# Moving one group of matmuls behind tile 0's last products in a projection that is called three times

## The reference

```
h = x + rms_norm(moba_attention(rms_norm(x)), ...)          # 8 heads; w_qkv, w_o
h = h + rms_norm(square(relu(rms_norm(h) @ w_up)) @ w_down)
h = h + gate * hgrn2_mixer(modulate(h))                      # linear recurrence; w_in, w_out
h = h + gate * swiglu(modulate(h))                           # ffn_w_in, ffn_w_out, layer 0
h = h + gate * nsa_mixer(modulate(h), shared_kv)             # 16 heads, 4 kv heads; w_q, w_kv, w_out
h = h + gate * swiglu(modulate(h))                           # layer 1
```

## Time and profile before

| | |
|---|---|
| time, median of 3 runs | 999.04 us (997.88 to 999.96) |
| the profiled execution's own time | 999.59 us |
| its span, from first to last instruction | 997.7 us |
| TensorE busy | 977.8 us, 98% |
| VectorE, ScalarE, POOL busy | 733.2, 521.7, 129.7 us |
| mean granted clock of TensorE | 0.999 |
| share of the last chain of waits | PE 79%, DVE 8%, DMA 5%, ACT 3% |

### The profile page before, as it was taken

The page is one execution under the profiler, slowest core; times in us unless marked ns, Lnnn a source line. Parts: engine busy times, 40 slices in busy tenths (PEclk is TensorE's granted clock), DMA queues, the critical chain, the costliest instruction groups (busy, mean ns, idle before and its releaser), DMA issues.

```text
span 997.7 us, 14897 instructions
## 1 busy us (share of the span) xinstructions
PE 977.8 (98%) x5482; PEld 800.0 (80%) x5482; DVE 733.2 (73%) x1086; ACT 521.7 (52%) x733; POOL 129.7 (13%) x163
## 2 busy tenths in 40 slices
PE   8999999999999999999999999999999999999998
PEld 6777788888887888887878888878877778888886
DVE  5787777787678979887878686999768876545454
ACT  6637375445455585873454344456277544434341
POOL 1000100000001000762400000014913120000000
PEclk9999999999999999999999999999999999999999
DMA  9991669799736979006799989658240328555541
GB/s 344 369 354 57 209 259 372 265 368 383 267 113 219 367 264 369 8 32 203 240 381 336 330 297 330 231 183 262 86 170 3 128 86 273 191 188 181 197 158 53
DMA packets 113796, 227.66 MB, mean 228 GB/s; under 512 B 5041, under 2 KB 58561, under 8 KB 113745
## 3 DMA queue, kind: packets, MB, share of 16 engines
q1 hardware_dynamic: 112192, 222.34, 62.2%
q0 software_dynamic: 1408, 4.54, 1.6%
q10 hardware_dynamic: 144, 0.10, 0.1%
HBM read 225.90 MB, written 1.06 MB: 227 GB/s over the span
## 4 chain that ended last, share of the span: by engine, by line
PE 79%; DVE 8%; DMA 5%; ACT 3%; issue 2%; SPq 1%; POOL 1%; DVEq 0%; ACTq 0%; POOLq 0%
PE psum L1980 74%; DMA adaw<-in_ada_w 2%; DVE wlo L1298 1%; DMA raw<-in_attn_w_qkv 1%; DMA raw<-in_ffn_w_in 1%; PE psum L2630 1%; DVE adaw L1319 1%; PE psum L2495 1%; PE psum L1998 1%; DVE arena L1418 1%; DMA raw<-in_attn_w_o 1%; ACT whi L791 1%; DVE res L1427 1%; PE psum L2358 1%; SPq L432 1%
## 5 line engine op out<-in xcount | busy, mean ns | idle before, releaser
L1298 DVE TENSOR_TENSOR wlo<-raw,whi 128x2048 fp32r<-128x2048 f32 (+1 forms) x156 | 310.3, 2005 | 137.4 <-ACT whi L791 137.1
L1980 PE MATMUL psum<-whi,xhi 128*128 128x512 f32 x888 | 350.7, 397 | 5.2 <-DVE xlo L1382 2.1
L1980 PE MATMUL psum<-whi,xlo 128*128 128x512 f32 x888 | 344.9, 390 | 0.0
L791 ACT CAST whi<-raw 128x2048 fp32r<-128x2048 f32 (+1 forms) x157 | 262.6, 1683 | 157.4 <-PE psum L1980 102.1
L1980 PE MATMUL psum<-wlo,xhi 128*128 128x512 f32 x888 | 343.4, 390 | 0.0
L1980 PEld LDWEIGHTS psum<-whi,xhi 128*128 128x128 f32 x888 | 166.7, 188 | 44.3 <-issue 6.5
L1980 PEld LDWEIGHTS psum<-whi,xlo 128*128 128x128 f32 x888 | 166.7, 188 | 35.5
L1980 PEld LDWEIGHTS psum<-wlo,xhi 128*128 128x128 f32 x888 | 166.9, 188 | 32.7
L1319 DVE SCALAR_TENSOR_TENSOR adaw<-adaw,crow 128x1024 f32<-128x1024 f32 x112 | 131.9, 1222 | 3.2 <-DMA adaw<-in_ada_w 3.0
L1980 PE MATMUL psum<-whi,hhi 128*128 128x512 f32 x296 | 115.4, 390 | 0.0
L1980 PE MATMUL psum<-whi,hlo 128*128 128x512 f32 x296 | 115.2, 389 | 0.0
(11 more groups left out here) (284 smaller groups left out, 987.4 us busy)
## 6 DMA issues: line engine op xcount, KB each, us to landing
adaw<-in_ada_w SPq DMA_DIRECT2D x48, 1024.0 KB, 6.9
raw<-in_ffn_w_in SPq DMA_DIRECT2D x88, 512.0 KB
raw<-in_ffn_w_out SPq DMA_DIRECT2D x44, 512.0 KB
raw<-in_w_up SPq DMA_DIRECT2D x16, 1024.0 KB
raw<-in_w_down SPq DMA_DIRECT2D x16, 1024.0 KB
raw<-in_hgrn_w_in SPq DMA_DIRECT2D x16, 1024.0 KB
raw<-in_attn_w_qkv SPq DMA_DIRECT2D x10, 1024.0 KB
adaw<-in_kv_ada_w SPq DMA_DIRECT2D x8, 1024.0 KB, 9.4
```

The costliest lines, as they stand in the source:

```text
L791: sc.copy(whi[:, s, 0:width], raw[:, s, 0:width]).then_inc(hi_ready[s], 1)
L1298: ve.tensor_tensor(wlo[:, s, 0:width], raw[:, s, 0:width], whi[:, s, 0:width].bitcast(F32), ALU.subtract).then_inc(lo_ready[s], 1)
L1980: return te.matmul(dst, lhsT, rhs, start=start, stop=stop, skip_group_check=open_)
```

## The change

In `accumulate` the second slot's products of tile 1, `part(1, 1)`, are issued between the two passes of the last loop instead of ahead of it. The order of the last five groups was: slot 1 tile 0, slot 1 tile 1, tile 0 slots 2 and 3, tile 1 slots 2 and 3. It becomes: slot 1 tile 0, tile 0 slots 2 and 3, slot 1 tile 1, tile 1 slots 2 and 3. The matmuls themselves, their operands and the semaphores that they raise are the same; `part(1, 1)` is what raises `used[1]`. Nothing changes on the other engines.

```
@@ -2120,8 +2120,9 @@
                 part(1, 0)
                 if late is not None:
                     late(3)
-                part(1, 1)
                 for i in range(TT):
+                    if i == 1:
+                        part(1, 1)
                     for f in range(2):
                         for s in (2, 3):
                             item_ready(s, n)
```

## The result

The changed kernel takes 1018.12 us (median of 4 runs, 1017.38 to 1019.91) against 999.08 before: 19.0 us more, ratio 1.0194 with a 95% interval of 1.0176 to 1.0212. It is slower, as forecast, by 19.0 instead of 16.5 us. The profiled execution has a span of 1016.9 us, 19.2 over the one before.

The account below looks back on a forecast made before the run. TensorE, busy for 98% of the span, was taken as the bound. Waits of 3.1 + 5.7 + 5.7 = 14.5 us plus 2.0 for one clock fall gave 16.5 us, 1015.5 on the median; range 1011.5 to 1019.5.

Parts of the forecast that it names:

- the queue behind `used[1]`: All three projections: late copy of slot 1 delays tile 0's post-processing in in-order lists, so TensorE waits; 14.5 us.
- First projection, 3.1 forecast: Attention output projection: TensorE waits 3.1 us at tile 0's transposes, behind slot 1's late copy and subtraction.
- Second, 5.7 for the copy: Recurrent mixer's projection: slot 1's copy, on the chain of waits, comes 5.44 + 0.3 late; cost 5.7 us.
- The price of a fall there, taken as 2.0: Second projection: clock falls during the wait, slowing eight transposes and six products; 2.0 us, the only fall counted.
- Third, 5.7 for the copy: Second attention's projection: copy 7.8 late, but VectorE's subtraction of slot 1 and the transposes 5.7 late; cost 5.7 us.
- The wait of 2.4 for slot 3: Third projection: tile 0's slot 3 products, wanted earlier, wait 2.4 us for VectorE's subtraction.
- The 2.4 is not added again: Third projection: the wait for slot 3 adds nothing to the 5.7 us, since the chain doesn't pass it twice.
- The rival with a fall in the third: Clock falls in the third projection too: 18.5 us, 1017.5; chance 0.27 for falls in more than one place.
- The rival with all three falls: Clock falls in all three projections, 1.0 us in the first: 19.5 us, 1018.5; within the same 0.27 chance.
- Downstream is rigid: MLP loops: each load and product is released by the one before, so delays aren't given back.
- The swallowing of the second's delay: Rival: a later load wait absorbs the second projection's 5.7 us; 8.8 us in all, 1007.8; chance 0.08.
- The rival on the other side: Faster: tile 0's sums, 2.7 us earlier, close TensorE's gaps before the transposes; 2.4 us gained, 996.6; chance 0.03.

Follow-up runs that it names:

- first_only: New order of products in the first projection only, the other two as in the kernel before: 1001.61 us, 3.6 over before.
- filled: Changed kernel plus products of constants in TensorE's long waits of the second and third projection: 1013.89 us, 15.9 over before.
- the changed kernel again: The changed kernel run once more without further edits, as base for comparisons: 1018.55 us, 20.1 over before.
- third_mended: Changed kernel with slot 1's copy and subtraction behind tile 0's post-processing, and the third's slot 3 subtraction ahead of the last turned low half: 998.93 us.
- lists_moved: Changed kernel with slot 1's copy (ScalarE) and subtraction (VectorE) moved behind tile 0's post-processing steps in all three projections: 1001.49 us, 3.1 over before.
- third_only: New order of products in the third projection only, the other two as in the kernel before: 1005.77 us, 7.8 over before.
- half: Against the kernel before, the moved group stands behind tile 0's first half of the columns only, in all three projections: 1006.34 us, 7.9 over before.

## Why the prediction was right, and where it was short

- What bounds the kernel, and the queue behind `used[1]`: right. Moving the two lists, with the new order of products kept, takes back 17 of 20 us.
- First projection, 3.1 forecast: 3.04 of idle in the profile, and 3.2 on the path (118.31 - 116.64 = 1.67, and the 1.5 by which the stretch began earlier). The run of its own gave 3.6, with an interval of 2.3 to 5.0 and a fall in it.
- Second, 5.7 for the copy: 5.8. Of the 0.3 in it for slot 3's late start only 0.1 was read from a row; the slot's products came 453.74 - 1.71 - 451.77 = 0.26 late. The price of a fall there, taken as 2.0: tile 1's transposes are 479.99 - 470.42 = 9.57 later and tile 0's 7.52, so 2.05. The load behind it took 10.51 us instead of 10.07, 0.4 that wasn't in the sum.
- Third, 5.7 for the copy: 7.2. The wait of 2.4 for slot 3 was forecast, and is 2.20. The step that was short is "The 2.4 is not added again", with the clock counted for the waits at the transposes alone. The prediction weighed standstills against the 2.7 us that the clock took to fall at the end of the kernel, and left this shorter one out. But behind this wait, too, the clock fell, and 30 products took 8.72 us instead of 7.10. That is 1.6 in front of the copy, where every us counts.
- "I count the fall in the second projection and leave the others to the rivals": the term that was too small. Behind the third's transposes it fell as well: 830.43 against 811.23 is 19.20, tile 0's 17.16, so 2.0. The rival with a fall in the third named 1017.5, without the one inside the stretch. In the profiled execution 2.05 + 1.6 + 2.0 = 5.7 us are the clock's, and 4.2 by the fillers over several executions; 2.0 had been forecast. The queue's part of the sum was right in size: 3.2 + 5.8 + 5.6 = 14.6, forecast 14.5.
- In the first, no fall was counted. The profiled execution had none (1.06 behind 3.04 us), but three others did (`first_only`, `filled`, the changed kernel again), for 0.5 to 1.4 us. The forecast's 1.0 for that fall was about right, its probability too low. The rival with all three falls named 1018.5, against 1018.12 measured. That closeness is partly luck: in the profiled execution its 1.0 in the first projection is missing, and 1.6 that it didn't have stands in the third.
- The sum of the profiled execution: 3.2 + 5.8 + 2.05 + 0.4 + 7.2 + 2.0 = 20.7, less 1.5 by which it reached the first projection earlier, is the 19.2 of the spans.
- Downstream is rigid, and the loads keep their distance: right. The swallowing of the second's delay didn't happen: the load wait moved from 488.64 to 498.21, by 9.57 like tile 1's transposes, and grew by 0.4.
- The rival on the other side, that the early sums close TensorE's gaps, failed on the lists as said. `third_mended`, where the lists no longer stand in the way, is worth at most 1.3 us by its interval, not 2.4. The gap before tile 1's transposes of the first projection stays (1.22 us). Those before tile 0's in the second and third (0.40 and 0.63 us by the brackets of the timeline before; the prediction's 0.56 was counted from start to start) do close, but behind them TensorE waits 0.47 and 0.45 us for tile 0's low halves, and in the third 0.86 us ahead of them.

## What to carry to other kernels

When a group of products is moved, look first at which semaphore its last product raises and at what stands behind the wait on it in the in-order lists of the other engines. Results that come earlier help only if the lists let them be used; results that come later can hold up everything behind the wait, related or not. Where two lists are coupled, change them together: the moved lists alone cost 4 us, the moved products alone 19, both together 3, and with slot 3's subtraction mended too nothing that can be measured. Here a wait of 2 to 6 us on TensorE cost, besides its own length on the path, up to 2 us more behind it through the clock, in some executions and not in others.

## What the runs showed of the hardware

- In the profiled executions a wait of 2.20 us was followed by a fall to 1.2 GHz in three (the changed kernel twice, `lists_moved`; 0.83 and then 0.50 in the windows behind the first) and by none in two (`third_only`, `half`; 1.00). One of 3.04 us in the first projection left the transposes at 1.06 us in one execution and made them 1.94 in three. One of 3.69 in the third left them at 1.06 in two and made them 1.94 in one. One of 3.11 in the second projection of `half` made them 1.26. Behind 5.82 or 5.83 they took 1.94 in all three.
- At the low level the transposes and six products took 1.94 + 2.58 = 4.52 instead of 1.06 + 1.41 = 2.47 us: 1.83 times as long, not twice. In the trace, the first products behind the transposes are 0.43 us apart instead of 0.23.

```profile
473.33 0.63 PE L1980 MATMUL psum<-whi,xlo 128*128 128x512 f32 x1
473.75 0.63 PE L1980 MATMUL psum<-whi,xhi 128*128 128x512 f32 x1
...
475.77 0.39 PE L1980 MATMUL psum<-whi,xhi 128*128 128x512 f32 x1
475.99 0.39 PE L1980 MATMUL psum<-wlo,xhi 128*128 128x512 f32 x1
```

- With 32 small products of constants in the wait of 5.8 us of the second projection the clock stayed at 1.00, and they delayed nothing, since they ended before the wait did (0.52 us of idle left).
